# Three seams of a transformer kernel: norm sums in the compressed-query stage, roots and splits of the first attention head, first triangles of the delta-rule scan

## What is computed

```python
h  = _modulate(_rms(x, norm_attn[l]), mod_x[0], mod_x[1])
qkv, z, beta_lg, decay_lg, cq, ckv, k_rope, gates = _split_in(h @ w_in[l])
qa, ka, va, g, beta = _gdn_inputs(qkv, beta_lg, decay_lg, conv_qkv[l], ...)   # conv of 5 taps, silu, l2norm
o_gdn, _, _ = _bidirectional_gdn(qa, ka, va, g, beta, s_fwd, s_bwd)
qb, kb, vb = _mla_qkv(cq, ckv, k_rope, mla_q_a_norm[l], mla_kv_a_norm[l], w_uq[l], w_ukv[l], q_norm[l], k_norm[l], (row, col))
o_mla = _blockwise_attention(qb, concat([kb_c, kb]), concat([vb_c, vb]))
x = x + mod_x[2] * _merge(_gdn_out(o_gdn, z, gdn_out_norm[l]), o_mla, gates, ...)
```

## Time and profile before

| | us |
|---|---|
| median of 3 runs | 2691.12 (2690.48 to 2693.11) |
| the profiled execution, its own time | 2688.22 |
| its span, from the first to the last instruction | 2686.1 |
| PE busy | 2580.8 (96% of the span) |
| DVE, POOL, ACT busy | 1656.5, 1179.5, 739.6 |
| mean granted clock of PE | 0.992 |

### The profile page before, as it was taken

One profiled execution on the slowest core, in us unless ns is written; L12 is line 12 of the kernel. 1 busy time (PEld: TensorE's weight loads), 2 busy tenths in 40 slices (PEclk: granted clock), 3 DMA queues, 4 the chain that ended last, 5 costly groups with the idle time before them and its releaser, 6 DMA issues. The chain is left out here.

```text
span 2686.1 us, 46243 instructions
## 1 busy us (share of the span) xinstructions
PE 2580.8 (96%) x18938; PEld 2166.5 (81%) x18938; DVE 1656.5 (62%) x2483; ACT 739.6 (28%) x1334; POOL 1179.5 (44%) x934
## 2 busy tenths in 40 slices
PE   8999999989899999999899989989899999999998
PEld 6878888878678888878788879876798888788887
DVE  7869759473568939758655566544687426562451
ACT  3224214110333404333544244322364100110000
POOL 3545555545335555533531253212443545454552
PEclk9999999999999999999999999999999999999999
DMA  4233333322023333322011111111111223222222
GB/s 162 94 110 141 131 136 136 105 93 97 1 79 145 138 132 139 113 71 79 27 42 47 51 41 27 34 38 51 49 30 48 96 97 106 72 101 94 94 94 78
DMA packets 51320, 229.74 MB, mean 86 GB/s; under 512 B 5296, under 2 KB 12480, under 8 KB 32576
## 3 DMA queue, kind: packets, MB, share of 16 engines
q1 hardware_dynamic: 51136, 227.10, 24.5%
HBM read 224.91 MB, written 2.17 MB: 85 GB/s over the span
## 5 line engine op out<-in xcount | busy, mean ns | idle before, releaser
L246 POOL TENSOR_TENSOR ring_rounded<-ring,ring_rounded 128x512 fp32r<-128x512 f32 (+2 forms) x711 | 950.8, 1368 | 1064.9 <-DVE ring_rounded L237 822.6
L300 PE MATMUL psum<-arena_rounded,ring_rounded 128*128 128x512 f32 (+1 forms) x2820 | 1093.2, 388 | 39.0 <-DVE arena_rounded L613 12.4
L301 PE MATMUL psum<-arena_rounded,ring_rounded 128*128 128x512 f32 (+1 forms) x2820 | 1083.7, 384 | 0.0
L302 PE MATMUL psum<-arena_rounded,ring_rounded 128*128 128x512 f32 (+1 forms) x2820 | 1083.5, 384 | 0.0
L300 PEld LDWEIGHTS psum<-arena_rounded,ring_rounded 128*128 128x128 f32 x2820 | 531.7, 189 | 157.7 <-issue 30.6
L302 PEld LDWEIGHTS psum<-arena_rounded,ring_rounded 128*128 128x128 f32 x2820 | 531.5, 188 | 106.0
L301 PEld LDWEIGHTS psum<-arena_rounded,ring_rounded 128*128 128x128 f32 x2820 | 532.1, 189 | 102.8 <-issue 1.0
L237 DVE CAST ring_rounded<-ring 128x2048 fp32r<-128x2048 f32 (+4 forms) x147 | 161.2, 1097 | 569.9 <-PE psum L302 521.8
L810 ACT ACTIVATE arena<-psum,vectors 128x512 f32<-128x512 f32 x88 | 68.0, 773 | 257.8 <-DVE psum L850 257.8
L701 DVE SCALAR_TENSOR_TENSOR arena<-arena 128x1024 f32<-128x1024 f32 x48 | 102.6, 2137 | 0.1
L2633 DVE TENSOR_TENSOR arena<-psum,lev 128x256 f32<-128x256 f32 x120 | 45.5, 420 | 91.4 <-PE psum L2349 91.1
(11 more groups left out here) (417 smaller groups left out, 3252.5 us busy)
## 6 DMA issues: line engine op xcount, KB each, us to landing
ring<-in_w_up SPq DMA_DIRECT2D x44, 1024.0 KB, 4.8
arena<-in_w_mod SPq DMA_DIRECT2D x48, 512.0 KB, 5.5
ring<-in_w_down SPq DMA_DIRECT2D x32, 704.0 KB, 4.1
ring<-in_w_mup SPq DMA_DIRECT2D x16, 1024.0 KB, 4.9
ring<-in_w_mdown SPq DMA_DIRECT2D x16, 1024.0 KB, 4.9
ring<-in_w_gdn SPq DMA_DIRECT2D x12, 1024.0 KB, 4.9
ring<-in_w_lru_in SPq DMA_DIRECT2D x10, 1024.0 KB, 4.9
ring<-in_w_odd_in SPq DMA_DIRECT2D x10, 1024.0 KB, 4.8
```

The source lines that it names most:

```text
L246: last = pool.tensor_tensor(self.rounded(low), raw, self.rounded(high).bitcast(F32), ALU.subtract)
L300: pe.matmul(out, r(wh), r(xh), start=start, stop=False)
L301: pe.matmul(out, r(wh), r(xl), start=False, stop=False)
L302: return pe.matmul(out, r(wl), r(xh), start=False, stop=stop)
```

## The change

**Scan's first triangles.** The triangles of tile 0 are made at the end of the input stage (class `FirstTriangle`). PE makes their products inside the last unit. ACT makes their eight Exp ahead of the last middle tap, DVE the triangles ahead of the last four outer taps, and POOL adds the identity at the end. PE's last `hold` grows from 24 to 40. In the scan stage `hold(11)`, the products, Exp and triangles of tile 0 go; the squares of the queries come behind the first two copies. Which bank serves which role for direction 0 changes.

```diff
@@ class FirstTriangle (new)
+    def act_decay(self, act, d):
+        m = self.m
+        act.wait_ge(m.sem("barred"), m.count("barred", d + 1))
+        for h in range(GH):
+            e = self.e[d][:, h, :]
+            last = act.activation(e, e, ACT.Exp, bias=scan_gcol(m, self.group, NEG_GC, SCAN_TILES[d][0], d, h))
+        last.then_inc(m.up("firstexp"), 1)
+
+    def dve_triangle(self, dve, d):
+        m, e = self.m, self.e[d]
+        dve.wait_ge(m.sem("firstexp"), m.count("firstexp", d + 1))
+        dve.wait_ge(m.sem("firstgram"), m.count("firstgram", d + 1))
...
@@ gdn_in_stage
+            if t == 1 and k == 3:
+                if bd:
+                    pe.wait_ge(m.sem("edec"), m.count("edec", 3))
+                pe.wait_ge(m.sem("freed"), m.count("freed", 9))
+                tri.pe_gram(pe, 0)
+                tri.pe_gram(pe, 1)
...
-        m.hold(pe, 24, 4)
+        m.hold(pe, 40, 4)
...
         silu(us[4], 0)
         silu(us[4], 1)
+        silu(us[5], 0)
+        tri.act_decay(act, 0)
+        tri.act_decay(act, 1)
         tap(us[5], 1)
-        silu(us[5], 0)
         silu(us[5], 1)
...
         key_roots()
         taps_of(us[5], 0)
+        tri.dve_triangle(dve, 0)
+        tri.dve_triangle(dve, 1)
         begin(us[5])
         taps_of(us[5], 1)
@@ gdn_scan_stage
-        decay(0, 0)
-        decay(0, 1)
-        for h in range(GH):
-            act.activation(qsq[h], qt[:, h, :], ACT.Square).then_inc(m.up("qsquare"), 1)
         for t in range(NA):
             x_copy(t, 0, 0)
             x_copy(t, 0, 1)
+            if t == 0:
+                for h in range(GH):
+                    act.activation(qsq[h], qt[:, h, :], ACT.Square).then_inc(m.up("qsquare"), 1)
```

```diff
+        products(us[1], 0, 0).then_inc(m.up("done"), 1)
         onorm.pe_sums(pe, 1)
...
+        products(us[1], 1, 0)
+        onorm.pe_turn(pe, 0)
+        onorm.pe_turn(pe, 1)
+        products(us[1], 1, 1).then_inc(m.up("done"), 1)
...
+        products(last, 0, 0)
+        onorm.pe_spread(pe, 0)
+        onorm.pe_spread(pe, 1)
+        pe.wait_ge(m.sem("summed"), m.count("summed", 2))
+        rstd_pe_sums(m, pe, qacc, NT, 7)
+        products(last, 0, 1).then_inc(m.up("done"), 1)
+        onorm.pe_spread(pe, 2)
+        onorm.pe_spread(pe, 3)
+        pe.wait_ge(m.sem("rstd"), m.count("rstd", 1))
...
```

```diff
                 for i in range(NA):
+                    if i == 3 and n == 11:
+                        turn_rows()
+                    if i == 3 and n == 12:
+                        spread_roots()
...
-        for unit in us[1:]:
+        for n, unit in enumerate(us[1:12], 1):
             m.pool_unit(pool, unit)
+            if n == 10:
+                pool.wait_ge(m.sem("rhalf"), m.count("rhalf", 1))
+                pool.wait_ge(m.sem("mean"), m.count("mean", 1))
+                pool.tensor_tensor(root, mean, rhalf, ALU.pow).then_inc(m.up("root"), 1)
+        for name, whole, high in (("qhigh", qn[:, 0, :], parts.qnh[0]), ("khigh", ka[:, 0, :], parts.knh[0]),
+                                  ("krhigh", parts.krl[0], parts.krh[0])):
+            pool.wait_ge(m.sem(name), m.count(name, 1))
...
+            last.then_inc(m.up("firstlow"), 1)
+        for unit in us[12:]:
+            m.pool_unit(pool, unit)
```

More of the change, by code:

```diff
@@ L2238, in gdn_scan_stage @@
     places = [512 * i for i in range(24)] + [VT_AT + 512 * i for i in range(2, 6)]
-    qsq = [m.at(places[24 + h], T) for h in range(GH)]
+    qsq = [m.at(places[i], T) for i in (26, 27, 8, 20)]
     qmean, qroot, qtmp = [m.small[:, a:a + GH * NT] for a in (Q_MEAN, Q_ROOT, Q_TMP)]
@@ L2909, in act @@
             act.activation(dst, outs[n], ACT.Square).then_inc(m.up("square"), 1)
+        for k in range(3):
+            act.wait_ge(m.sem("qnormed"), m.count("qnormed", k + 1))
+            act.activation(m.rounded(cqh[:, k, :]), cql[:, k, :], ACT.Copy).then_inc(m.up("qnhigh"), 1)
     def dve(dve):
@@ L3029, in turn, with turn_rows, spread_roots @@
             pe.matmul(m.psum[:, 6, :], m.at(ROT_AT, P), qr[:, j, :], start=True, stop=True).then_inc(m.up("rotated"), 1)
+        def turn_rows():
+            pe.wait_ge(m.sem("krowed"), m.count("krowed", 2))
+            for i in range(NT + NA):
+                last = pe.transpose(m.psum[:, 7, 8 * i:8 * i + 8], rows(i), m.ident[0:8, 0:8])
+            last.then_inc(m.up("rcols"), 1)
+        def spread_roots():
+            pe.wait_ge(m.sem("rstd"), m.count("rstd", 1))
+            for j in range(NA):
+                pe.matmul(m.psum[:, 6, j * P:(j + 1) * P] if j < NT else
+                                 m.psum[:, 7, (j - 2) * P:(j - 1) * P],
+                                 root[:, 8 * (NT + j):8 * (NT + j) + 1].broadcast_to([P, P]), m.ident[:, :],
+                                 start=True, stop=True)
+            pe.transpose(m.psum[0:8 * NA, 7, 0:P], root[:, 8 * NT:], m.ident[:, :]).then_inc(m.up("rootrows"), 1)
         qhalves = lambda k: (cqh[:, k, :], cql[:, k, :])
@@ L3066, in pe @@
                         turn(i - 8)
-            if n == 11:
-                pe.wait_ge(m.sem("krowed"), m.count("krowed", 2))
-                for i in range(NT + NA):
-                    last = pe.transpose(m.psum[:, 7, 8 * i:8 * i + 8], rows(i), m.ident[0:8, 0:8])
-                last.then_inc(m.up("rcols"), 1)
-        pe.wait_ge(m.sem("rstd"), m.count("rstd", 1))
-        pe.transpose(m.psum[0:8 * NA, 7, 0:P], root[:, 8 * NT:], m.ident[:, :]).then_inc(m.up("rootrows"), 1)
-        m.hold(pe, 11, 6)
     def act(act):
@@ L3107, in dve, with root_mean @@
+        act.wait_ge(m.sem("kscaled"), m.count("kscaled", 1))
+        act.activation(m.rounded(parts.knh[0]), ka[:, 0, :], ACT.Copy).then_inc(m.up("khigh"), 1)
+        act.wait_ge(m.sem("krscaled"), m.count("krscaled", 1))
+        act.activation(m.rounded(parts.krh[0]), parts.krl[0], ACT.Copy).then_inc(m.up("krhigh"), 1)
+        act.wait_ge(m.sem("done"), m.count("done", 2 * 12 + 2))
+        act.wait_ge(m.hi_done, us[12].g + 2)
+        m.act_unit(act, us[12])
     def dve(dve):
         c = m.vchain
+        def root_mean():
+            dve.wait_ge(m.sem("rcols"), m.count("rcols", 1))
+            dve.tensor_scalar(mean, m.psum[:, 7, 0:8 * (NT + NA)], 1.0 / (QK_N + ROPE), EPS, ALU.mult,
+                              ALU.add).then_inc(m.up("mean"), 1)
@@ new lines, in root_newton, with first_keys @@
+        def root_newton():
+            dve.wait_ge(m.sem("root"), m.count("root", 1))
+            rstd_newton(m, dve, mean, root, tmp, m.sig("rstd"))
+            dve.wait_ge(m.sem("rstd"), m.count("rstd", 1))
+            dve.tensor_scalar(root[:, 0:8 * NT], root[:, 0:8 * NT], float(QK_N + ROPE) ** -0.5, None,
+                              ALU.mult).then_inc(c.up(), 1)
+        def first_keys():
+            dve.wait_ge(m.sem("rootrows"), m.count("rootrows", 1))
+            row = ((slice(0, T), m.psum[:, 6, :]), (CTX, m.psum[:, 7, TC:T]))
+            for cols, r in row:
+                last = dve.tensor_tensor(ka[:, 0, cols], ka[:, 0, cols], r, ALU.mult)
+            last.then_inc(m.up("kscaled"), 1)
+            for cols, r in row:
+                last = dve.tensor_tensor(parts.krl[0][:, cols], kr[:, cols], r, ALU.mult)
+            last.then_inc(m.up("krscaled"), 1)
+            dve.wait_ge(m.sem("qrhigh"), m.count("qrhigh", 1))
+            high = m.rounded(parts.qrs[:, 0, :])
+            dve.tensor_tensor(high[OTHER, :], qr[ROPED, 0, :], high[ROPED, :].bitcast(F32),
+                              ALU.subtract).then_inc(m.up("qrlow"), 1)
+            dve.tensor_copy(turned_row, m.psum[0:8 * NA, 7, 0:P]).then_inc(m.up("rowsout"), 1)
@@ L3160, in dve @@
                 kv_low(1)
-            dve.wait_ge(m.sem("done"), m.count("done", 2 * n + 2))
-            m.dve_unit(dve, unit)
             k_ = kind(n)
```

323 lines of the change are left out of this document (184 added, 139 removed).

## The result

The changed kernel takes 2704.66 us (median of 6 runs, 2703.99 to 2708.54), the kernel before in the same series 2691.57 (2684.63 to 2694.63). The ratio is 1.0054, with a 95% interval of 1.0044 to 1.0064: slower by about 13 us. The forecast was 2705.0 and its range 2692 to 2713.

A forecast was written before the change was run, and what follows sets the result against it. PE was busy nearly all of the 2686.1 us span, so seams were judged by their last-ending chain. +9.3 - 4.5 + 9.1 = +13.9 us took the profiled 2688.2 to 2702.1, with the 2.9 offset 2705; range 2692 to 2713.

The forecast's parts named there:

- Part C: Heads to attend: all heads' roots by POOL power, head 0 prepared in the heads stage, attend begins with a score; +9.1 us.
- the power: Heads stage, POOL: `pow` of 80 columns, 0.158 us each and 0.4 besides, takes 13.0 us, bounds 12 and 16.
- The walk from the root to the first score: End of heads: Newton step, spreads, keys, halves, POOL's split last, from 1907.8 to 1925.6; first score +5.1 us.
- The rows' stall: Start of attend: DVE waits for head 1's key rows, read only at the stage's start; +4.0 us, bounds 0 and 5.5.
- Part B: Compressed-query stage: norm sums and spreads placed between products; -4.5 us, bounds -6 and -2.5.
- The waits of 2.31 and 1.05: Compressed-query stage: PE's waits for the second squares, 2.31 us, and between spreads, 1.05 us, both go.
- the new one: Compressed-query stage: first spread waits for the eviction of unit 1, 0.7 us left over, bounds 0 and 2.
- Part A: Input to scan, both groups: first triangles made in the input stage; +9.3 us.
- The seam chain: Input to scan: masks, Exp, triangles, last taps, silu, load; seed 9.8 us behind masks, +2.5 and +1.8 us by group.
- 1.5 us for the squares: Scan start: PE waits for ACT's squares ahead of the query sums; +1.5 us in each group, bounds 1 to 1.7.
- 1.0 for the clock: Behind the scan's seed: granted clock falls to half after PE idles; +1.0 us in each group, bounds 0 and 1.7.
- 0, if POOL delivers earlier: Input-to-scan seam, each group: lower bound of the seed's delay, 0, if POOL's masks come earlier; upper bound +4.

The follow-up runs named there:

- the run with early rows: Heads-to-attend change alone, with square root for the power and head 1's key rows read in the heads stage, against the kernel before: 2686.21 us, ratio 0.9982.
- part B alone: Kernel before with only the compressed-query stage changed, norm sums, turns and spreads placed between products: 2685.40 us, ratio 0.998.
- the changed kernel with the square root: Whole changed kernel with only the power of 80 columns put back to square root and reciprocal: 2690.71 us against 2690.70 before, ratio 1.0003.
- part A alone: Kernel before with only the scan's first triangles moved into the input stages, with its scan banks and squares: 2703.42 us against 2691.20, ratio 1.0040.
- The early masks: First-triangles change alone, with POOL's masks ahead of its weight split and ACT's decays earlier, against the kernel before: 2697.22 us against 2692.04, ratio 1.0023.
- the kernel with the square root: Heads-to-attend change alone, with ACT square root and DVE reciprocal in place of POOL's power, against the kernel before: 2687.80 us, ratio 0.9991.
- the kernel without part A and all else mended: Kernel before plus the compressed-query change and the heads change with square root, early rows and moved weight split, no first triangles: 2677.75 us, ratio 0.9956.

## Why the prediction was right, and where it was not

The sum held: +13.9 forecast, +13.1 measured. Its parts:

**Part C, forecast +9.1, alone +8.7.** The step that carried it was the power, extrapolated from two sizes to 13.0 us; it took 13.15. These were not the two nearest sizes, as the rows call them: the same trace has a power of 24 columns at 5.01 us and another of 32 at 6.27, each 0.8 us above the line through the two rows. The bounds of 12 and 16 had room for that, but the forecast doesn't mention it, and hitting 13.15 so closely is partly luck. The walk from the root to the first score was put at 17.8 us and took 18.15 (1920.40 to 1938.55), with the expected last work, POOL's split. Counted from the start of the heads stage the first score came 5.9 us later, forecast 5.1. The rows' stall was sized at 4.0; the rest of attend is 2.5 longer, of a wait of 2.85, and the run with early rows shows that 1.8 of 3.0 such us are on the path. So one term was too small by 0.8 and one too large by 1.5. The exchange of the one operation for 12.1 us settles the mechanism. The Trainium skill's page GPSIMD Engine Reference, section 3.1, gives about 2.6 cycles an element, measured on an add. By that rate, as an estimate, the power would be under 1 us; the 13.15 us show that it doesn't hold for `pow`.

**Part B, forecast -4.5, alone -5.8 (stage -4.9).** The waits of 2.31 and 1.05 went; the new one was 0.57 where 0.7 was taken. In part B alone the low clock of the earlier trace rows at 1766 left the stage, as forecast, but stood at the start of the next one, where it cost 1.6 us; in the changed kernel with the square root it is in neither, and the stage is -4.9 there too. In the changed kernel a slice lies at the stage's start:

```profile
1766.00:1770.00 4.00, 3.69 (x10) 2.94 (x11) 4.00 (x6) 4.00 (x6) 0.00 (x0) 0.57 1.02 411
```

That is the difference between -4.9 and -3.3.

**Part A, forecast +9.3, alone +12.2.** The seam chain was right step by step: the seed 9.80 us behind the masks' end (forecast 9.8), in group 1 9.79. Counted from the start of their input stages, the seeds are 2.8 and 1.8 us later than before in the changed kernel, forecast 2.5 and 1.8; in group 0 of part A alone it is 2.5. The next step failed in its make-up: I added 1.5 us for the squares to 1.0 for the clock in each group. They are not two costs in a row but partly two covers of the same stretch. The squares cost 1.35 us where the clock is full, close to the 1.5, but PE's wait for them is only 0.26 and 0.70 in the changed kernel, where it is low. Taking the low clock away gave 0.4 us back in group 0 and 2.0 in group 1. The sum of the two, 2.5 for a first tile, came out as 2.4 and 1.0 in the changed kernel and 2.8 and 2.2 in part A alone, so in three of four tiles about the right size came from a wrong split, which is luck. What the forecast lacked is the rest of the scan, which I took as unchanged: 1.8 and 0.8 us in part A alone, 3.8 and 2.7 in the changed kernel's profiled execution. In that one the fourth tile of group 0 took 33.13 us where it had been 29.97, and one of its slices was at the low clock. Other runs on record bear on it. The changed kernel with the square root has the same scan code, and its rest of the scan is 142.1 and 142.0 us, where before has 143.1 and 140.9. The seven profiled kernels without part A, whose scan code is all the same, range from 142.1 to 144.3 and from 140.7 to 143.2. So the 3.8 and 2.7 are mostly that execution's. Whether part A adds a little to the rest of the scan stays open, and with it why its median is 2.9 above the forecast.

The early masks also answer a question that the prediction left at "0, if POOL delivers earlier" as the lower bound for a seam. Each input stage gained 1.8 us by it. The seed of group 0, counted from the start of its input stage, is then 0.7 us later than before. That of group 1 comes after 110.1 us, as in part B alone, where the old code has its input stage free of the low clock too. So the bound of 0 was right as a bound, and DVE is what lies beneath.

## What to carry to other kernels

Price a function by its own rows, at its own size, before moving it: a `pow` on POOL that takes 1.1 us on 4 columns takes 13 on 80, and a square root on ACT with a reciprocal on DVE did the same work in 0.9 us and one table load. When a stage ends in a barrier, ask of every engine what its last instruction is and who needs it; a weight split that nobody wanted for over a hundred microseconds held the stage for 4.5 us. Moving a head's preparation into the stage ahead pays only if an engine there is idle: PE had nothing to give, DVE was full, and the triangles' 4.9 us only changed their address, while what had been covered (squares, rows, a warm clock) lost its cover. And a full clock is worth what the next waits leave of it: 0.4 us at one seed, 2.0 at the other.

## What the runs showed of the hardware

- **`pow` on POOL** goes by the column: 1.1 us for 4, 2.9 for 16, 5.4 for 32, 13.15 for 80 of float32, some 0.158 us each. The powers of 24 columns (5.01) and one of 32 (6.27) lie 0.8 us above that line; why, no run shows. An ACT square root of the same 80 columns is 0.27 us, DVE's reciprocal 0.64, the table load 1.28. ACT, then DVE, in the kernel with the square root:

```profile
1897.95 1.28 ACT L3141 ACT_TABLE_LOAD   x1
1899.24 0.27 ACT L3141 ACTIVATE small<-small 128x80 f32<-128x80 f32 x1
...
1900.59 0.64 DVE L3160 RECIPROCAL small<-small 128x80 f32<-128x80 f32 x1
```

- **The low clock wanders.** PE's granted clock fell to 1.2 GHz for short slices at seams, but not at the same ones in each kernel. In the kernel before the mean of a window was 0.57 at 1766 to 1770 us and 1.00 at 1812 to 1816, the start of the heads stage. In part B alone the slice lay at that start, 0.58, and took 1.6 us of untouched code (heads +1.6 in the table):

```profile
1807.00:1811.00 4.00, 3.41 (x8) 2.74 (x9) 2.44 (x3) 1.58 (x2) 2.69 (x2) 0.58 0.33 98
```

  A slice cost 1.3 to 1.6 us in stages that differ in nothing else (input stage of group 1, compressed-query, heads, attend), but not everywhere. One at 1927 us in attend of the kernel with the square root cost nothing: from the second maximum to the fourth it is 7.32 us, and 7.33 in the kernel without part A and all else mended, which has the full clock there. So the profiled stages of two kernels can differ by that much with no cause in the edit, and a pair of profiles alone would have put +20.6 us on this change.
- **A small read of rows is slow however early it is asked for.** The 128 KB and 256 KB spreads of a key row over the partitions landed 5.7 to 7.3 us after their issue in the mended kernel without part A, before and behind the stage's end alike. By these figures it takes an issue more than 7 us ahead of the use to hide them; with the first at 1903.40 and the use wanted at 1908.8 they came 2.45 us late.
- **DVE and POOL disturb each other on small work.** DVE's operation of 24 columns with two inputs from SBUF takes 0.17 us alone and 1.30 beside a POOL operation of 1.28; in the changed kernel the first Newton product of 80 columns took 1.29 beside a piece of POOL's split that began 0.06 ahead of it. In the kernel with the square root it took 0.28, although POOL was at work there too, on a piece that had begun 1.1 us ahead of it. The Trainium skill says why, in SBUF — State Buffer, section SBUF: two separate sides: the two engines share one pair of ports, whoever starts first holds it for the whole instruction, and a DVE operation with two inputs from SBUF needs it. The 1.30 and 1.29 agree: they are as long as one POOL instruction. The 0.28 agrees only in part, since POOL's piece ended 0.18 us behind its start.
